# Two-layer hybrid decoder trunk: the steps from w_o to the layer's end in an order of their own for each engine, and the seven products in the order P1 P7 P2 P6 P3 P5 P4

## The chip, the core and the metric

One core of one Trainium2 chip runs the whole kernel. The metric is the device time of one execution, in microseconds (us). Below, PE is TensorE (matmuls), DVE is VectorE, ACT is ScalarE, SP is SyncE (it only issues transfers here).

## The reference

```python
for l in range(2):                                   # x: 512 tokens x 1024
    u = rms_norm(x, norm1_w[l])
    proj = u @ w_in[l]                               # projections of three branches, and gates
    ybr = stack([short_conv(...), gated_linear_attention(...), sliding_window_attention(...)])
    branch = einsum('bsgc,gcd->bsgd', ybr, w_branch[l])
    mixed = sum(sigmoid(gates) * branch, axis=2)
    x = x + mixed @ w_o[l]
    h = rms_norm(x, norm2_w[l])
    x = x + square(relu(h @ w_up[l])) @ w_down[l]    # w_up 1024 x 4096, w_down 4096 x 1024
```

All is float32. The change touches each layer from `mixed @ w_o` to its end.

## The kernel before

**Split products.** PE multiplies in a rounded 32-bit form. So each operand is split into a high part and the remainder, and each product is three matmuls: high by high, low by high, high by low. For every weight tile ACT writes the high part (`split_high`, L767) and then DVE the remainder (`split_low`, L984). A *unit* is the work on one such tile of 128x1024: 24 matmuls for a unit of w_up (`up0` to `up31` in a layer) or of w_o (`wa0`-`wa3`, `wb0`-`wb3`), 12 for one of w_down (`dn0` to `dn55`). The split tiles lie in four slots (`SPLIT`), so the split of a unit waits until the unit four before it is done, and PE waits for `lo_done` before each unit. Before, each engine's loop calls `split_ahead` at fixed places: at the step of unit n it splits unit n+3.

**The MLP.** The hidden width of 4096 is done in four quarters. In a quarter PE does eight `up` units (the hidden activations, transposed, one accumulator each) and then 14 `dn` units. ACT takes each `up` result through relu and square (L942, L944) and writes its high part; DVE writes the remainder (`hidden_low`). The product of a quarter's hidden activations with its 1024 rows of w_down is done by seven products of half-size blocks (a Winograd form of Strassen's scheme) in place of eight: for each product i (0 to 6 in the code) two units, one for each pair of w_down row blocks. Four of the weight operands are sums of blocks that DVE makes in place in `raw_down` (L1366): b12 = b22 - b12, b11 = b12 + b11, then b21 = b21 - b11, b11 = b22 - b11. Three of the left operands are sums of hidden blocks (`hidden_sums`: L1348, L1350, L1352, rounded by ACT in L930, remainders L1361) and one a difference (`hidden_diff`, L1342).

**The order of a quarter, before.** The products are taken in the order of i, so the units `dn2`, `dn3` are the second product. DVE makes b12 and b11 at the steps of up6 and up7, and b21 and b11 again at `dn2`, `dn3`. Each product's result is taken from its accumulators by `down_result` two units later: three products go to x directly (L1370, scaled by a norm factor for each token), four are kept over the quarters in `product_sums` (L1385, L1387) and are combined and added to x in the last quarter. All are lines of one loop for each engine; there is no scheduler. Within an engine's queue the instructions run in program order, and a wait holds all behind it.

**Banks.** Each product takes two of the four accumulators, the next product the other two; PE opens them again when DVE has taken the result of the product before the last.

**Transposes.** x is transposed on PE for the norms: V0-V7 between the attention part and the MLP (after `wb1` and after `up1`), UT4-UT7 for the next layer after the unit `dn54`.

**Transfers.** SP issues w_up in slabs of two units (1 MB, two slots, `raw_free`), and after the four slabs of a quarter the quarter's w_down: two halves (`down_full[0]`, `down_full[1]`) of two 1 MB transfers each, once `down_free` says that the last quarter's half has been split.

## Time and profile before

| what | value |
|---|---|
| median of the runs shown (3 runs, 1687.06 to 1688.86) | 1687.3 us |
| the profiled execution's own time | 1687.93 us |
| span of its trace | 1686.1 us |
| PE busy | 1604.5 us (95%) |
| DVE busy | 1060.4 us (63%) |
| ACT busy | 727.8 us (43%) |
| mean granted TensorE clock | 0.984 |
| DMA, mean over the span | 90 GB/s |

Busy times are shares of the span of the trace; the device time is 1.8 us longer. A matmul's record lasts longer than the distance to the next one (they are pipelined), so PE's progress is read from counts in a stretch, not from the duration of one.

### The profile page before, as it was taken

To read this page: it belongs to the slowest core of one execution; us is meant where nothing else is said; L and a number is where in the kernel's file an instruction comes from. 1 tells how busy PE (TensorE), PEld (TensorE's weight loads), DVE (VectorE), ACT (ScalarE), POOL (GpSimd) and SP (SyncE) were. 2 spreads that over 40 slices of the span, in tenths; PEclk is the share of its full clock that TensorE was granted. 3 is DMA by queue.
4 is the path that set the end of the run, shared out by engine and by line. 5 is a ranking of instruction groups with operands and counts; after the bars stand their busy time and mean duration, and the time that the engine had idled before them with its cause. 6 is when DMAs were issued, how large, how long until landed. Compare 5 with 4: busy or idle time off the path is not lost.

```text
span 1686.1 us, 20623 instructions
## 1 busy us (share of the span) xinstructions
PE 1604.5 (95%) x7488; PEld 1306.2 (77%) x7488; DVE 1060.4 (63%) x1508; ACT 727.8 (43%) x1128; POOL 0.2 (0%) x4
## 2 busy tenths in 40 slices
PE   6999999999998989999789999999999989898987
PEld 4878778888887877778577877788888868787875
DVE  4566774554548677675966666655455494857668
ACT  4546552322254453535345465432233544534451
POOL 0000000000000000000000000000000000000000
PEclk9999999999999999999999999999999999999999
DMA  4321222332341412214012213133223504040301
GB/s 142 104 97 51 75 76 76 100 123 77 108 169 48 146 54 100 101 50 155 1 58 93 76 52 99 51 100 125 75 75 125 196 5 175 25 175 25 141 10 50
DMA packets 107572, 151.09 MB, mean 90 GB/s; under 512 B 4912, under 2 KB 81232, under 8 KB 107472
## 3 DMA queue, kind: packets, MB, share of 16 engines
q1 hardware_dynamic: 107040, 149.69, 26.7%
q8 instruction: 60, 0.98, 0.2%
q14 instruction: 40, 0.33, 0.1%
q10 hardware_dynamic: 432, 0.08, 0.0%
HBM read 147.67 MB, written 2.10 MB: 89 GB/s over the span
## 4 chain that ended last, share of the span: by engine, by line
PE 78%; DVE 12%; ACT 4%; DVEq 2%; issue 2%; SPq 1%; DMA 0%; ACTq 0%
PE acc L478 17%; PE acc L479 16%; PE acc L480 16%; PE acc L500 5%; PE acc L502 5%; PE acc L501 5%; DVE raw_down L1366 4%; PE acc L527 3%; PE acc L528 3%; PE acc L529 3%; DVE wl_rows L984 3%; ACT wh_rows L767 2%; DVEq L1431 1%; DVE x_tokens L1370 1%; PE bank L664 1%
## 5 line engine op out<-in xcount | busy, mean ns | idle before, releaser
L478 PE MATMUL acc<-uh,wh 128*128 128x512 f32 x1152 | 453.6, 394 | 7.2 <-DVEq L1001 7.1
L480 PE MATMUL acc<-uh,wl 128*128 128x512 f32 x1152 | 449.5, 390 | 0.0
L479 PE MATMUL acc<-ul,wh 128*128 128x512 f32 x1152 | 449.5, 390 | 0.0
L984 DVE TENSOR_TENSOR wl<-raw,wh 128x1024 fp32r<-128x1024 f32 x144 | 176.3, 1225 | 171.7 <-ACT wh L767 163.7
L478 PEld LDWEIGHTS acc<-uh,wh 128*128 128x128 f32 x1152 | 216.9, 188 | 58.1 <-DVE wl L984 7.8
L480 PEld LDWEIGHTS acc<-uh,wl 128*128 128x128 f32 x1152 | 216.8, 188 | 45.9
L479 PEld LDWEIGHTS acc<-ul,wh 128*128 128x128 f32 x1152 | 216.9, 188 | 43.8
L767 ACT ACTIVATE wh<-raw 128x1024 fp32r<-128x1024 f32 x144 | 152.0, 1056 | 174.2 <-PE acc L480 83.9
L767 ACT ACTIVATE wh_rows<-raw_down 128x1024 fp32r<-128x1024 f32 x112 | 114.9, 1051 | 129.0 <-DVE raw_down L1366 69.6
L984 DVE TENSOR_TENSOR wl_rows<-raw_down,wh_rows 128x1024 fp32r<-128x1024 f32 x112 | 136.9, 1222 | 38.1 <-ACT wh_rows L767 34.8
L527 PE MATMUL acc<-wh_rows,hidden_hi 128*128 128x512 f32 x192 | 83.3, 434 | 37.3 <-DVE wl_rows L984 37.2
L1010 DVE TENSOR_TENSOR gate_tanh<-acc,rsqrt_rows 128x512 f32<-128x512 f32 x48 | 33.2, 691 | 115.7 <-PE acc L480 115.5
L500 PE MATMUL acc<-wh_rows,uh 128*128 128x512 f32 (+1 forms) x256 | 97.4, 381 | 6.7 <-DVE swa_qk_tokens L1098 6.4
L915 ACT ACTIVATE gate_tanh<-gate_tanh 128x512 f32<-128x512 f32 x40 | 25.3, 633 | 171.7 <-DVEq L1011 171.7
L502 PE MATMUL acc<-wl_rows,uh 128*128 128x512 f32 (+1 forms) x256 | 94.4, 369 | 0.0
L501 PE MATMUL acc<-wh_rows,ul 128*128 128x512 f32 (+1 forms) x256 | 94.3, 368 | 0.0
L942 ACT ACTIVATE hidden<-acc 128x512 f32<-128x512 f32 x64 | 38.3, 598 | 125.9 <-PE acc L480 125.9
L527 PE MATMUL acc<-wh_rows,hidden_sums_hi 128*128 128x512 f32 x192 | 77.1, 402 | 11.2 <-DVE x_tokens L1370 6.0
L1366 DVE TENSOR_TENSOR raw_down<-raw_down 128x1024 f32<-128x1024 f32 x64 | 78.4, 1225 | 6.1
L528 PE MATMUL acc<-wh_rows,hidden_lo 128*128 128x512 f32 x192 | 81.3, 423 | 0.0
L529 PE MATMUL acc<-wl_rows,hidden_hi 128*128 128x512 f32 x192 | 80.8, 421 | 0.0
L527 PEld LDWEIGHTS acc<-wh_rows,hidden_hi 128*128 128x128 f32 x192 | 40.0, 208 | 50.4 <-DVE wl_rows L984 41.0
(212 smaller groups left out, 2433.7 us busy)
## 6 DMA issues: line engine op xcount, KB each, us to landing
raw<-in_w_in_dram SPq DMA_DIRECT2D x40, 1024.0 KB, 5.2
raw<-in_w_up_dram SPq DMA_DIRECT2D x32, 1024.0 KB, 5.6
raw_down<-in_w_down_dram SPq DMA_DIRECT2D x32, 1024.0 KB, 11.1
raw_branch<-in_w_in_dram SPq DMA_DIRECT2D x12, 1024.0 KB, 5.0
raw_branch<-in_w_branch_dram SPq DMA_DIRECT2D x12, 1024.0 KB, 5.0
raw_branch<-in_w_o_dram SPq DMA_DIRECT2D x8, 1024.0 KB, 5.0
x_tokens<-in_x_dram SPq DMA_DIRECT2D x4, 512.0 KB, 5.2
raw_kv<-in_w_in_dram SPq DMA_DIRECT2D x4, 512.0 KB, 3.6
```

Of the source, the lines that this page charges most:

```text
L478: nc.tensor.matmul(a[:], wh[slot][:, k, :], right_h, start=at_k == 0, stop=False)
L479: nc.tensor.matmul(a[:], wh[slot][:, k, :], right_l, start=False, stop=False)
L480: last = nc.tensor.matmul(a[:], wl[slot][:, k, :], right_h, start=False, stop=at_k == n - 1)
L500: nc.tensor.matmul(to, left_h[:, k, s], h[:, row, 0:cols], start=k == 0, stop=False)
L501: nc.tensor.matmul(to, left_l[:, k, s], h[:, row, 0:cols], start=False, stop=False)
L502: last = nc.tensor.matmul(to, left_h[:, k, s], lo[:, row, 0:cols], start=False, stop=k == KT - 1)
L527: nc.tensor.matmul(to[:], left[0], h[:, row, :], start=k == 0, stop=False)
L528: nc.tensor.matmul(to[:], left[1], h[:, row, :], start=False, stop=False)
L529: last = nc.tensor.matmul(to[:], left[0], lo[:, row, :], start=False, stop=k == BK - 1)
L767: nc.scalar.activation(split_view(True, u), raw_view(u), ACT.Copy).then_inc(hi_done, 1)
L984: V.tensor_tensor(split_view(False, u), raw_view(u), split_view(True, u).bitcast(f32), ALU.subtract).then_inc(lo_done, 1)
L1366: return V.tensor_tensor(to, a, b, op)
```

## The change

The four loops of the late part are replaced by three written-out lists of steps (`PE_LATE`, `ACT_LATE`, `DVE_LATE`), which each engine walks on its own. In them `+u` is the split of unit u, `rl`/`hh` are relu with square and the high part, `hl` the remainder, `su`/`sh`/`sl` the sums of hidden blocks with their high and low part, `df`/`dh`/`dl` the same for the difference, `ta`, `tb`, `tc`, `td` the four sums of w_down blocks (for each half), `rs` the taking of one accumulator of a product, `fo` the combining of the kept sums, `ra`/`rb` the residual of w_o, `gc` a copy of an accumulator by ACT. A DVE step begins with a drain (the engine finishes what it has begun). The products run as i = 0, 4, 1, 2, 5, 3, 6. On SP the two halves of w_down are issued between the slabs of the quarter. The combining of the kept sums moves from the last quarter's results to its `up` steps, from sums without the last quarter, and the last products are then added to each of the x tiles that they belong to.

```diff
+PRODUCT = (0, 4, 1, 2, 5, 3, 6)
+PE_LATE = """wa0 wa1 wa2 wa3 wb0.01 V0 wb0.2 V1 wb0.3 V2 wb1.0 V3 wb1.123 wb2 wb3 up0.0 V4 up1.0 V5 up2.0 V6 up3.0 V7 up0.1 up1.1
...
+dn42 dn43 dn44 dn45 dn46 dn47 dn48 dn49 dn50 dn51 dn52 dn53 dn54 dn55.0 UT4 dn55.1 UT5 UT6 UT7""".split()
...
                     for i in range(8 * q, 8 * q + 8, 2):
                         load(l, f"up{i}", rows(w_up, l, 0, KT, i * P, SLAB_COLS))
-                    for pair in range(PAIRS):
-                        sp.wait_ge(down_free[pair], l * QUARTERS + q + 1)
...
+                        pair = i % 8 // 2 - 1
+                        if pair in range(PAIRS):
+                            sp.wait_ge(down_free[pair], l * QUARTERS + q + 1)
...
+                def fold(i):
+
+                    g1, g6, g5, g7 = (g[:] for g in gsum)
+                    if i == 1:
+                        V.tensor_tensor(g6, g6, g1, ALU.add)
+                        V.drain().then_inc(folded, 1)
+                    elif i == 3:
+                        V.tensor_tensor(g7, g7, g6, ALU.add)
+                    else:
+                        row, half, part = {0: (0, 0, g1), 2: (0, 1, g6), 4: (1, 1, g7), 5: (1, 0, g7),
+                                           6: (0, 1, g5), 7: (1, 1, g5)}[i]
+                        for t in range(2):
+                            scaled_into_x(row, t, half, part[:, t, :])
+
+                def down_last(place, t):
...
+                    if i == 0:
+                        dve.wait_ge(g1_ready, 2 * l + t + 1)
+                        scaled_into_x(0, t, 0, a[:]).then_inc(free, 1)
+                    elif i == 2:
+                        V.tensor_tensor(g1, g1, a[:], ALU.add).then_inc(free, 1)
+                        V.drain()
+                        for row, half in ((0, 1), (1, 1), (1, 0)):
+                            scaled_into_x(row, t, half, g1)
+                    else:
+                        tiles = {1: ((0, 0),), 3: ((0, 1), (1, 1)), 4: ((1, 1), (1, 0)), 5: ((0, 1),), 6: ((1, 0),)}[i]
+                        for row, half in tiles:
+                            last = scaled_into_x(row, t, half, a[:])
+                        last.then_inc(free, 1)
...
+                for word in DVE_LATE:
+                    kind, i = step_of(word)
                     V.drain()
```

In `DVE_LATE` the second quarter of a layer reads, from up15 to the start of the next quarter: `+up15 dl1 +dn14 tb2 su4 hl12 +dn15 tb3 su5 hl13 sl4 su6 hl14 sl5 +dn16 sl6 +dn17 su7 rs14 rs15 hl15 sl7 +dn18 +dn19 +dn20 rs16 rs17 +dn21 tc2 +dn22 rs18 rs19 td2 +dn23 tc3 td3 +dn24 rs20 rs21 +dn25 rs22 rs23 +dn26 +dn27 rs24 +up16`. The last quarter reads, from dn46 on: `+dn46 rs42 hl31 rs43 +dn47 +dn48 rs44 rs45 +dn49 sl15 +dn50 rs46 rs47 tc6 rs48 td6 +dn51 tc7 rs49 td7 +dn52 rs50 +dn53 +dn54 rs51 +dn55 rs52 rs53 +gq0 +gq1 +gk0 UT4 UT5 UT6 UT7 rs54 rs55`.

What stands in DVE's queue in the second quarter of the first layer, before: from the split of dn16 (`wl_rows_70`; the four slots are 70 to 73 in turn, `raw_down_127` and `128` are the two halves of w_down). The rows of hidden sums and remainders that repeat are left out.

```order
L984 TENSOR_TENSOR wl_rows_70<-raw_down_127,wh_rows_66 128x1024
L1366 TENSOR_TENSOR raw_down_128<-raw_down_128 128x2x512 x2
...
L1361 TENSOR_TENSOR hidden_sums_lo<-hidden_sums,hidden_sums_hi 128x768 x2
L984 TENSOR_TENSOR wl_rows_71<-raw_down_128,wh_rows_67 128x1024
L984 TENSOR_TENSOR wl_rows_72<-raw_down_127,wh_rows_68 128x1024
L1366 TENSOR_TENSOR raw_down_127<-raw_down_127 128x2x512 x2
L1387 TENSOR_TENSOR product_sums_122<-product_sums_122,acc 128x512 x2
L984 TENSOR_TENSOR wl_rows_73<-raw_down_128,wh_rows_69 128x1024
L1366 TENSOR_TENSOR raw_down_128<-raw_down_128 128x2x512 x2
```

The first row is the split of dn16, the next split (`wl_rows_71`) that of dn17; between them stand two block sums and all of the last three hidden blocks. The same place in the changed kernel, from the split of dn16 to that of dn22:

```order
L1013 TENSOR_TENSOR wl_rows_70<-raw_down_127,wh_rows_66 128x1024
L1453 TENSOR_TENSOR hidden_sums_lo<-hidden_sums,hidden_sums_hi 128x768
L1013 TENSOR_TENSOR wl_rows_71<-raw_down_128,wh_rows_67 128x1024
...
L1013 TENSOR_TENSOR wl_rows_72<-raw_down_127,wh_rows_68 128x1024
L1013 TENSOR_TENSOR wl_rows_73<-raw_down_128,wh_rows_69 128x1024
L1013 TENSOR_TENSOR wl_rows_70<-raw_down_127,wh_rows_66 128x1024
L1362 TENSOR_TENSOR product_sums_125<-product_sums_125,acc 128x512 x2
L1013 TENSOR_TENSOR wl_rows_71<-raw_down_128,wh_rows_67 128x1024
L1465 TENSOR_TENSOR raw_down_127<-raw_down_127 128x2x512
L1013 TENSOR_TENSOR wl_rows_72<-raw_down_127,wh_rows_68 128x1024
```

Only one remainder stands between the splits of dn16 and dn17 now, and of the second pair of block sums the first (L1465) comes between the splits of dn21 and dn22. The first block sum of a half, b12, is now made at the `up` steps.

DVE in the last quarter of the first layer, before, from the split of dn50 (`wl_rows_72`) to that of dn52 (`wl_rows_70`); `product_sums_122` to `125` are the four kept sums.

```order
L984 TENSOR_TENSOR wl_rows_72<-raw_down_127,wh_rows_68 128x1024
L1387 TENSOR_TENSOR product_sums_123<-product_sums_123,acc 128x512
L1370 SCALAR_TENSOR_TENSOR x_tokens<-product_sums_123,rsqrt_tokens_mlp_sq,x_tokens 128x512
L1396 TENSOR_TENSOR product_sums_125<-product_sums_125,product_sums_123 128x512
L1387 TENSOR_TENSOR product_sums_123<-product_sums_123,acc 128x512
L1370 SCALAR_TENSOR_TENSOR x_tokens<-product_sums_123,rsqrt_tokens_mlp_sq,x_tokens 128x512
L1396 TENSOR_TENSOR product_sums_125<-product_sums_125,product_sums_123 128x512
L984 TENSOR_TENSOR wl_rows_73<-raw_down_128,wh_rows_69 128x1024
L984 TENSOR_TENSOR wl_rows_70<-raw_down_127,wh_rows_66 128x1024
```

Between the splits of dn50 and dn51 stand the six operations of one product's result, and none between those of dn51 and dn52. The same place in the changed kernel, DVE again, from the split of dn50 to that of dn52:

```order
L1013 TENSOR_TENSOR wl_rows_72<-raw_down_127,wh_rows_68 128x1024
L1347 SCALAR_TENSOR_TENSOR x_tokens<-acc,rsqrt_tokens_mlp_sq,x_tokens 128x512 x2
L1465 TENSOR_TENSOR raw_down_127<-raw_down_127 128x2x512
L1387 TENSOR_TENSOR product_sums_122<-product_sums_122,acc 128x512
L1347 SCALAR_TENSOR_TENSOR x_tokens<-product_sums_122,rsqrt_tokens_mlp_sq,x_tokens 128x512 x3
L1467 TENSOR_TENSOR raw_down_127<-raw_down_127 128x2x512
L1013 TENSOR_TENSOR wl_rows_73<-raw_down_128,wh_rows_69 128x1024
L1465 TENSOR_TENSOR raw_down_128<-raw_down_128 128x2x512
L1387 TENSOR_TENSOR product_sums_122<-product_sums_122,acc 128x512
L1347 SCALAR_TENSOR_TENSOR x_tokens<-product_sums_122,rsqrt_tokens_mlp_sq,x_tokens 128x512 x3
L1467 TENSOR_TENSOR raw_down_128<-raw_down_128 128x2x512
L1013 TENSOR_TENSOR wl_rows_70<-raw_down_127,wh_rows_66 128x1024
```

Four block sums of 128x1024 (L1465, L1467), which stood ahead of these splits before, are now among them, with the ten operations of two results.

## Rows read from the trace of the kernel before

**Rows 1.** The page, part 1: PE's busy time, share and instructions.

```profile
PE 1604.5 (95%) x7488; PEld 1306.2 (77%) x7488; DVE 1060.4 (63%) x1508; ACT 727.8 (43%) x1128; POOL 0.2 (0%) x4
```

**Rows 2.** Who PE waited for: us in total, times, longest us.

```profile
PE acc L527 <- DVE wl_rows L984: 43.5, 15, 4.6
```

**Rows 3.** Stretches: us, busy (x instructions) of PE, PEld, DVE, ACT, POOL, PEclk, DMA, GB/s.

```profile
436.54:481.84 45.30, 45.30 (x209) 37.74 (x208) 23.10 (x26) 12.85 (x15) 0.00 (x0) 1.00 0.37 116
481.84:572.99 91.15, 85.83 (x377) 70.17 (x376) 65.36 (x87) 47.01 (x63) 0.00 (x0) 0.98 0.25 86
572.99:662.05 89.06, 84.02 (x361) 68.47 (x360) 60.72 (x71) 40.23 (x51) 0.00 (x0) 0.98 0.27 95
662.05:751.42 89.37, 83.81 (x361) 68.35 (x360) 60.71 (x71) 40.21 (x51) 0.00 (x0) 0.98 0.27 94
751.42:856.24 104.82, 91.10 (x377) 73.08 (x376) 76.20 (x91) 42.94 (x55) 0.00 (x0) 0.93 0.24 84
...
1315.49:1406.65 91.16, 85.65 (x377) 70.10 (x376) 65.37 (x87) 47.06 (x63) 0.00 (x0) 0.98 0.24 85
1406.65:1495.73 89.08, 84.76 (x362) 69.48 (x361) 60.63 (x71) 40.33 (x51) 0.00 (x0) 0.96 0.27 94
1495.73:1585.11 89.38, 84.74 (x362) 69.30 (x361) 60.72 (x71) 40.33 (x51) 0.00 (x0) 0.96 0.27 95
1585.11:1682.44 97.33, 86.37 (x361) 68.38 (x359) 69.51 (x84) 36.95 (x48) 0.00 (x0) 0.96 0.20 75
```

**Rows 4.** Stretches of two quarters: the up units, and the product units (columns as above).

```profile
572.99:616.51 43.52, 43.52 (x193) 36.04 (x192) 20.90 (x26) 22.16 (x32) 0.00 (x0) 1.00 0.52 185
616.51:662.05 45.54, 40.50 (x169) 32.43 (x168) 39.81 (x46) 18.06 (x20) 0.00 (x0) 0.96 0.04 9
...
794.94:856.24 61.30, 47.58 (x185) 37.04 (x184) 55.30 (x66) 20.78 (x24) 0.00 (x0) 0.89 0.03 9
```

**Rows 5.** Timeline of PE: start, us, line, operation, [idle before <-releaser].

```profile
540.06 0.50 PE L527 MATMUL acc<-wh_rows,hidden_hi 128*128 128x512 f32 x1 [4.61 <-DVE wl_rows L984]
...
821.85 0.47 PE L527 MATMUL acc<-wh_rows,hidden_sums_hi 128*128 128x512 f32 x1 [1.68 <-DVE x_tokens L1370]
...
849.10 0.45 PE L543 MATMUL bank<-consts,x_tokens 128*128 128x128 f32 x1 [4.59 <-DVEq L1405]
```

**Rows 6.** Stretches behind two of these waits (columns as in rows 3).

```profile
540.00:542.00 2.00, 1.94 (x6) 1.50 (x7) 1.77 (x3) 0.06 (x1) 0.00 (x0) 0.63 0.00 0
820.00:830.00 10.00, 8.32 (x37) 6.68 (x36) 8.95 (x12) 4.84 (x5) 0.00 (x0) 1.00 0.00 0
```

**Rows 7.** Timeline of DVE around the wait at 540.06.

```profile
535.42 0.42 DVE L1350 TENSOR_TENSOR hidden_sums<-hidden_sums,hidden 128x256 f32<-128x256 f32 x1
...
536.44 0.69 DVE L1355 TENSOR_TENSOR hidden_lo<-hidden,hidden_hi 128x512 fp32r<-128x512 f32 x1
537.05 1.82 DVE L1361 TENSOR_TENSOR hidden_sums_lo<-hidden_sums,hidden_sums_hi 128x768 fp32r<-128x768 f32 x2
538.79 2.53 DVE L984 TENSOR_TENSOR wl_rows<-raw_down,wh_rows 128x1024 fp32r<-128x1024 f32 x2
541.46 2.52 DVE L1366 TENSOR_TENSOR raw_down<-raw_down 128x1024 f32<-128x1024 f32 x2
543.90 1.28 DVE L1385 COPY product_sums<-acc 128x512 f32<-128x512 f32 x2
545.10 1.21 DVE L984 TENSOR_TENSOR wl_rows<-raw_down,wh_rows 128x1024 fp32r<-128x1024 f32 x1
...
550.22 1.41 DVE L1370 SCALAR_TENSOR_TENSOR x_tokens<-acc,rsqrt_tokens_mlp_sq,x_tokens 128x512 f32<-128x512 f32 x2
```

**Rows 8.** Groups of instructions by line and form: busy us, mean ns of one.

```profile
L767 ACT ACTIVATE wh_rows<-raw_down 128x1024 fp32r<-128x1024 f32 x112 | 114.9, 1051 | 129.0 <-DVE raw_down L1366 69.6 <-PE acc L529 59.3
L942 ACT ACTIVATE hidden<-acc 128x512 f32<-128x512 f32 x64 | 38.3, 598 | 125.9 <-PE acc L480 125.9
L944 ACT ACTIVATE hidden<-hidden 128x512 f32<-128x512 f32 x64 | 40.5, 633 | 5.2
```

**Rows 9.** The page, part 6, transfers: line engine op xcount, KB each, us to landing.

```profile
raw_down<-in_w_down_dram SPq DMA_DIRECT2D x32, 1024.0 KB, 11.1
```

394 lines of the change are left out of this document (195 added, 199 removed).

## The prediction

> **What bounds the kernel now.** I read the page first: PE is busy 95% of the span [rows 1], so only what keeps PE from starting matmuls can move the end. Second, PE's waits: the largest is for DVE's remainders of w_down tiles, 43.5 us in 15 waits [rows 2]. Third, where they lie. In the up units of a quarter 192 matmuls take 43.52 us [rows 4], 0.2267 us each: that is PE without a wait. So an up unit takes 5.44 us and a dn unit of 12 matmuls 2.72 us, and a quarter (8 and 14 of them, 360 matmuls) would take 81.6 us. It takes 89.06 and 89.37 us in the middle of a layer [rows 3]: 7.46 and 7.77 us lost, all among the dn units (45.54 us for 38.08 us of matmuls [rows 4]). The first quarter has 16 transposes more. Their price is in the row of w_o, 45.30 us for 192 matmuls and 16 transposes [rows 3], so 45.30 - 43.52 = 1.78 us; then 91.15 - 81.6 - 1.78 = 7.77 us are lost. In all, the six quarters that are not a layer's last lose 7.77 + 7.46 + 7.77 + 7.78 + 7.48 + 7.78 = 46.0 us. The last quarters take 104.82 (with 16 transposes) and 97.33 us [rows 3]: 21.4 and 15.7 us lost.
>
> The timeline shows why. PE stands 4.61 us before `dn3` at 540.06 [rows 5], and DVE has no pause there: sums, remainders and splits follow each other [rows 7]. A quarter's dn part holds 39.81 us of DVE work in 45.54 us, its up part only 20.90 in 43.52 [rows 4]. So the bound is an uneven load on DVE: too much work stands before the splits of dn2 and dn3. Behind the wait the granted clock is 0.63 in 540 to 542 [rows 6], so it has gone down to 1.2 GHz for a part of it; `dn3` then takes 4.67 us (540.06 to 544.73, the last matmul's slot included) in place of 2.72, 1.95 us more. Behind a wait of 1.68 us the clock stays at 1.00 [rows 5, 6].
>
> **The change, costed by walking the two queues.** Durations from the rows. A DVE operation on 128x1024 behind a drain starts 1.31 us after the one before ([rows 7]: two splits at 538.79, the next at 541.46); the drain thus adds 0.085 to 1.225. So I take 0.77 us for one accumulator's copy or add, 0.51 for each step of a hidden sum, 0.77 for a remainder of 128x512, 1.03 for one of a hidden sum, 0.83 for a scaled addition to x (1.49 for two in a row). An ACT split is 1.05 us [rows 8], 1.1 with its drain; relu and square 0.60 and 0.63 [rows 8], 1.4 together.
>
> *A middle quarter*, from the first matmul of up8 = 0. PE without waits ends up15 at 43.5 and starts dn14+j at 43.5 + 2.72 j. Until dn16 DVE is early: the list has b12 (`ta2`, `ta3`) among the up units. The chain that sets the rest: up15 ends 43.5, ACT splits dn17, relu and square until 46.0, DVE's `su7` until 47.5, then the results of the first product (its second tile is done with dn15 at 49.0) until 49.8, `hl15` 50.6, `sl7` 51.6, and three splits in a row, dn18 52.9, dn19 54.2, dn20 55.5. PE wants these at 54.4, 57.1, 59.8. On with the list: two results 57.1, dn21 58.4, `tc2` 59.7, dn22 61.0 (wanted 65.3), two results 62.6, `td2` 63.9, dn23 65.2, `tc3` `td3` 67.8, dn24 69.1 (wanted 70.7), results 70.7, dn25 72.0 (73.4), results 73.6, dn26 74.9 (76.2), dn27 76.2 (78.9), then up16 78.3 (81.6). No split is late, the smallest margin is 1.3 to 1.6 us. The accumulators are taken in time too: the sixth product opens its first at 70.7, where `rs20` ended at 69.9. The other five non-last quarters give the same by the same walk (in the first, `hl7` ends at 52.7 where dn5 wants it at 59.0). So 46.0 us go.
>
> *A last quarter.* Its results cost more: 24 additions of one tile in the dn part and twelve half-rows plus two adds of 128x1024 among the up units, where there is room. By the walk DVE has dn46 at 49.3 (wanted 54.4), dn48 at 54.4 (59.8), dn50 at 61.0 (65.3). Then two results 62.7, `tc6` 64.0, one result of add and three scaled additions (0.77 + 0.66 + 0.66 + 0.83 = 2.9) 67.0, `td6` 68.3, dn51 69.7: wanted 68.0, **1.7 us late**. `tc7` 71.0, the second such result 73.9, `td7` 75.2, dn52 76.5: PE would now want it at 72.4, **4.1 us late**. All later splits are in time. So 5.8 us of waits, and as 4.1 is near the 4.61 behind which the clock fell, I add its 1.95 us: the quarter takes 81.6 + 5.8 + 1.95 = 89.3 us. In layer 1 that is 97.33 - 89.3 = 8.0 us won. In layer 0 the transposes add 1.78 and the first unit of the next layer waits some 0.4 for the remainders of UT5 to UT7: 104.82 - 91.5 = 13.3 us won; the wait of 4.59 us before the transposes at 849.10 [rows 5] goes, since DVE ends the last right-hand x tile at 85.5 in my walk and PE reaches the transposes at 88.
>
> *Against it*: the groups of 16 transposes are cut into fours, each return to 128x512 matmuls costs about 0.1 us (1.78 / 16 = 0.11 for all of a transpose is the upper bound), 12 more returns: 1.2 us. Below it is nothing. I take 1.2.
>
> *At nothing*: more drains on ACT (727.8 us busy of 1686 [rows 1]; its queue is waited for only where DVE is not late); 1.0 us for the two `gc` copies, hidden before dn47; the earlier issue of the w_down halves. Four 1 MB transfers in a row land in 11.1 us each [rows 9]; the second half is issued about 1.6 us before up8 starts and so lands by 9.5, while `ta3` is reached at about 9 and holds the split of up13, wanted at 5 x 5.44 = 27.2. With 1.31 us for `ta3` and 1.31 for the split a landing up to 24.6 costs nothing: a cover of 15 us.
>
> *The sum*: 46.0 + 8.0 + 13.3 - 1.2 = 66.1 us. 1686.1 - 66.1 = 1620.0 us of span, plus the 1.8 us between span and device time 1621.8; the profiled run is 0.6 us above the median, so **1621 us**.
>
> **A rule weighed.** In the list each accumulator is taken as a step of its own behind a drain; before, the two of a product ran in a row, both done 1.20 us after the first began (543.90, the next split at 545.10 [rows 7]), 0.60 us each. With drains I count 0.77, so 14 x 0.17 = 2.4 us more DVE work in a quarter. The Trainium skill (VectorE: DVE Perf Modes, "The DRAIN you can't avoid") says the pipe is flushed after every operation anyway and that leaving out waits between them wins nothing. By it the list's drains would be free: about 2.4 us less lateness in each last quarter, 1616 us in place of 1621. The row speaks against it, so I keep 0.77.
>
> **The rivals.**
> - *A: the last quarters lose little.* Should DVE be some 2.4 us earlier than in my walk, the wait at dn52 is under 2 us and the clock stays up, as at 821.85. Then each last quarter gains 2.4 + 1.95 = 4.35 us more: 1621 - 8.7 = 1612 us. For it: the margins are sums of twenty terms, and one that is 0.1 too large makes 2 us. Against: the terms are measured.
> - *B: short waits in every quarter.* The margins of 1.3 us in the middle quarters are of the same size as that error. If every one of the six keeps a wait of 2 us and half of a fall of the clock with it, they lose 6 x 3, and a last quarter 3 more each: 1621 + 24 = 1645 us.
> - *C: slower.* The queue of DVE holds `ta3` ahead of the splits of up13 and up14. If the second half of w_down landed late, all splits behind would be late. It costs nothing up to a landing 24.6 us after the quarter starts, and the change loses as much as it wins (66 / 8 = 8.2 us in each quarter) at 32.8. Landing at 36 would give 1687 + 8 x 3.2 = 1713 us. Against it: 24.6 is far above the 9.5 expected, with the DMA engines 0.52 busy in the up part [rows 4].
> - *D: no change.* If the waits were due to something that the lists keep (PE's own start behind `lo_done`), the time stays near 1687. Rows 7 show DVE without a pause there, so hardly.
>
> **How the numbers follow.** The forecast (1615 to 1628) 0.50, A and below 0.20, B 0.24, C 0.03, D 0.03. The time predicted is the forecast's. The range 1608 to 1640 takes in A with both last quarters good, and most of B: what lies outside is a quarter of B, a part of A, C and D, under 0.2. A measurement of this kernel tells a change from none at about 0.2% (3.4 us). Faster by more: forecast, A and B, 0.94; same 0.02, most of D; slower 0.04, C and the rest of D.
>
> **What the profile after would show.** Right: stretches of 360 matmuls in 81.6 to 82 us between the first up units of two middle quarters, with no wait for `wl_rows` and the clock at 1.00 in them; in the last quarter two waits, before dn51 and dn52; no wait before UT4. DVE's busy time in the up part goes up, in the dn part down. The prediction is wrong if a middle quarter still shows waits (B), if PE waits before an up unit with DVE standing at the first sum of w_down blocks (C), or if a last quarter's dn part takes 38 to 40 us (A).

## The result, and the profile after

The changed kernel takes 1625.72 us (median of 4 runs, 1625.26 to 1626.25) against 1687.22 us (1687.06 to 1688.86) before: a ratio of 0.9634, with a 95% interval of 0.9617 to 0.9650. The forecast was 1621 us, the range 1608 to 1640. The profiled execution took 1625.36 us, its span 1623.6. The steps have the same names; only line numbers moved (a split on VectorE is L1013 now, a product's matmuls L570 to L572, `tc` L1465, `td` L1467, a scaled addition to x L1347).

The page, part 1, then PE's waits of the whole span (us in total, times, longest us), answering to [rows 1, 2]:

```profile
PE 1584.9 (98%) x7488; PEld 1296.4 (80%) x7488; DVE 1088.6 (67%) x1524; ACT 745.5 (46%) x1132; POOL 0.2 (0%) x4
```

```profile
PE acc L570 <- DVE wl_rows L1013: 11.2, 4, 3.9
PE bank L587 <- DMA x_tokens<-in_x_dram: 9.9, 1, 9.9
PE acc L520 <- DVEq L1030: 7.2, 1, 7.2
...
PE acc L570 <- DVE product_sums L1360: 0.2, 1, 0.2
```

Fifteen waits of 43.5 us for the remainders of w_down blocks have become four of 11.2. The next two rows are of the start of the program, before the first product (9.93 to 20.62 us). Gone are also six waits for results that VectorE had not yet taken from their accumulators; PE's waits before:

```profile
PE acc L527 <- DVE x_tokens L1370: 6.0, 6, 1.7
```

PE's own busy time went down too, by 19.6 us; fewer matmuls at the low clock were part of it (the mean granted clock is 0.992 in this execution).

The stretches that answer to [rows 3] (w_o and the four quarters of layer 0, then the quarters of layer 1):

```profile
436.02:481.44 45.42, 45.42 (x210) 37.62 (x209) 24.52 (x27) 15.28 (x18) 0.00 (x0) 1.00 0.56 193
481.44:565.24 83.80, 83.80 (x378) 69.06 (x377) 64.72 (x85) 47.36 (x61) 0.00 (x0) 1.00 0.22 72
565.24:646.84 81.60, 81.60 (x362) 67.59 (x361) 62.74 (x71) 41.87 (x51) 0.00 (x0) 1.00 0.30 101
646.84:728.64 81.80, 81.80 (x361) 67.51 (x360) 62.32 (x71) 41.88 (x51) 0.00 (x0) 1.00 0.31 107
728.64:821.63 92.99, 86.78 (x377) 71.03 (x376) 82.73 (x96) 44.44 (x55) 0.00 (x0) 0.96 0.22 74
...
1282.28:1366.27 83.99, 83.79 (x378) 69.05 (x376) 64.71 (x86) 47.35 (x61) 0.00 (x0) 1.00 0.22 72
1366.27:1447.87 81.60, 81.60 (x362) 67.57 (x360) 62.76 (x71) 41.85 (x51) 0.00 (x0) 1.00 0.30 101
1447.87:1530.03 82.16, 82.12 (x362) 67.41 (x360) 62.81 (x71) 41.88 (x51) 0.00 (x0) 1.00 0.31 105
1530.03:1620.13 90.10, 85.09 (x361) 69.37 (x359) 78.56 (x93) 39.89 (x50) 0.00 (x0) 0.96 0.18 64
```

Two quarters are exactly 360 matmuls long, 81.60 us, with the clock at 1.00 and PE busy all the time. The halves of the second and of the last quarter of layer 0 show how the work moved (compare [rows 4]):

```profile
565.24:608.76 43.52, 43.52 (x194) 36.05 (x193) 28.21 (x35) 24.28 (x33) 0.00 (x0) 1.00 0.44 146
608.76:646.84 38.08, 38.08 (x170) 31.54 (x169) 34.53 (x37) 17.59 (x18) 0.00 (x0) 1.00 0.14 50
728.64:772.16 43.52, 43.52 (x193) 36.04 (x192) 39.41 (x48) 24.21 (x33) 0.00 (x0) 1.00 0.45 148
772.16:821.63 49.47, 43.26 (x185) 34.99 (x184) 43.33 (x48) 20.22 (x23) 0.00 (x0) 0.93 0.03 8
```

VectorE has 28.21 us of work among the up units where it had 20.90, and 34.53 among the product units where it had 39.81. That is 3.5 us less than the 38.08 us that PE's matmuls take: it fits.

The last quarter has the two waits that were expected, before dn51 and dn52. PE's timeline, then VectorE's, then the clock in stretches (columns as in rows 3):

```profile
799.15 0.50 PE L570 MATMUL acc<-wh_rows,hidden_sums_hi 128*128 128x512 f32 x1 [2.35 <-DVE wl_rows L1013]
...
806.03 0.80 PE L570 MATMUL acc<-wh_rows,hidden_sums_hi 128*128 128x512 f32 x1 [3.86 <-DVE wl_rows L1013]
806.63 0.63 PE L571 MATMUL acc<-wh_rows,hidden_sums_lo 128*128 128x512 f32 x1
```

```profile
797.87 1.23 DVE L1013 TENSOR_TENSOR wl_rows<-raw_down,wh_rows 128x1024 fp32r<-128x1024 f32 x1
799.19 1.23 DVE L1465 TENSOR_TENSOR raw_down<-raw_down 128x1024 f32<-128x1024 f32 x1
800.50 0.69 DVE L1387 TENSOR_TENSOR product_sums<-product_sums,acc 128x512 f32<-128x512 f32 x1
801.28 2.08 DVE L1347 SCALAR_TENSOR_TENSOR x_tokens<-product_sums,rsqrt_tokens_mlp_sq,x_tokens 128x512 f32<-128x512 f32 x3
803.44 1.23 DVE L1467 TENSOR_TENSOR raw_down<-raw_down 128x1024 f32<-128x1024 f32 x1
804.75 1.23 DVE L1013 TENSOR_TENSOR wl_rows<-raw_down,wh_rows 128x1024 fp32r<-128x1024 f32 x1
```

```profile
804.00:806.00 2.00, 0.00 (x0) 0.00 (x0) 1.89 (x2) 1.17 (x2) 0.00 (x0) 0.78 0.00 0
806.00:808.00 2.00, 1.97 (x5) 1.58 (x6) 1.84 (x2) 1.86 (x2) 0.00 (x0) 0.50 0.00 0
808.00:810.00 2.00, 2.00 (x6) 1.56 (x5) 1.81 (x3) 0.14 (x1) 0.00 (x0) 0.50 0.00 0
810.00:812.00 2.00, 2.00 (x6) 1.57 (x5) 1.52 (x2) 0.38 (x1) 0.00 (x0) 0.51 0.00 0
812.00:814.00 2.00, 2.00 (x10) 1.64 (x10) 0.81 (x2) 0.68 (x1) 0.00 (x0) 1.00 0.00 0
```

Between the splits of dn51 (797.87) and dn52 (804.75) VectorE has no pause: `tc7`, the result `rs49` with its three scaled additions, `td7`. PE stands 3.86 us, the granted clock falls to 0.50 (1.2 GHz), and the next matmuls are 0.63 us long where they would be 0.39 or 0.40.

### The profile page after: what moved, and what is told of

Same layout as the page of the kernel before. It is cut to its first block, busy times and chain, and to the rows that moved or that the text cites. A ratio compares the mean times of both kernels' runs of the same rounds, so it can differ in the third digit from the quotient of the medians.

```text
span 1623.6 us, 21215 instructions
## 1 busy us (share of the span) xinstructions
PE 1584.9 (98%) x7488; PEld 1296.4 (80%) x7488; DVE 1088.6 (67%) x1524; ACT 745.5 (46%) x1132; POOL 0.2 (0%) x4
## 4 chain that ended last, share of the span: by engine, by line
PE 92%; DVE 5%; ACT 1%; DVEq 1%; SPq 1%; issue 0%; DMA 0%; ACTq 0%
PE acc L520 19%; PE acc L522 19%; PE acc L521 19%; PE acc L570 5%; PE acc L572 5%; PE acc L571 5%; PE acc L542 5%; PE acc L544 5%; PE acc L543 5%; DVE wl_rows L1013 2%; PE bank L708 1%; PE bank L727 1%; DVE x_tokens L1347 1%; PE bank L587 1%; PE bank L719 1%; PE bank L666 1%
## 5 line engine op out<-in xcount | busy, mean ns | idle before, releaser
L521 PEld LDWEIGHTS acc<-ul,wh 128*128 128x128 f32 x1152 | 216.8, 188 | 43.5
L1013 DVE TENSOR_TENSOR wl<-raw,wh 128x1024 fp32r<-128x1024 f32 x144 | 176.3, 1225 | 68.7 <-ACT wh L799 57.4
L799 ACT ACTIVATE wh_rows<-raw_down 128x1024 fp32r<-128x1024 f32 x112 | 118.9, 1061 | 153.1 <-DVE raw_down L1467 65.7
L1013 DVE TENSOR_TENSOR wl_rows<-raw_down,wh_rows 128x1024 fp32r<-128x1024 f32 x112 | 137.2, 1225 | 15.8 <-ACT wh_rows L799 6.1
L570 PE MATMUL acc<-wh_rows,hidden_sums_hi 128*128 128x512 f32 x192 | 78.1, 407 | 11.4 <-DVE wl_rows L1013 11.2
L799 ACT ACTIVATE wh_rows<-raw_branch 128x1024 fp32r<-128x1024 f32 x40 | 42.3, 1059 | 76.3 <-PE acc L544 66.4
L571 PE MATMUL acc<-wh_rows,hidden_sums_lo 128*128 128x512 f32 x192 | 76.8, 400 | 0.0
L572 PE MATMUL acc<-wl_rows,hidden_sums_hi 128*128 128x512 f32 x192 | 76.7, 399 | 0.0
L570 PE MATMUL acc<-wh_rows,hidden_hi 128*128 128x512 f32 x192 | 75.0, 390 | 0.0
L572 PE MATMUL acc<-wl_rows,hidden_hi 128*128 128x512 f32 x192 | 74.7, 389 | 0.0
L571 PE MATMUL acc<-wh_rows,hidden_lo 128*128 128x512 f32 x192 | 74.7, 389 | 0.0
```

Source lines behind the costliest of these rows:

```text
L521: nc.tensor.matmul(a[:], wh[slot][:, k, :], right_l, start=False, stop=False)
L570: nc.tensor.matmul(to[:], left[0], h[:, row, :], start=k == 0, stop=False)
L571: nc.tensor.matmul(to[:], left[1], h[:, row, :], start=False, stop=False)
L572: last = nc.tensor.matmul(to[:], left[0], lo[:, row, :], start=False, stop=k == BK - 1)
L799: nc.scalar.activation(split_view(True, u), raw_view(u), ACT.Copy).then_inc(hi_done, 1)
L1013: V.tensor_tensor(split_view(False, u), raw_view(u), split_view(True, u).bitcast(f32), ALU.subtract).then_inc(lo_done, 1)
```

## The experiments

Each kernel is the changed one with the edit shown. Where a median is given, it is of four or five runs, or more, on a chip on which the kernel before was timed as well (1687.5 to 1687.8 us). e1 to e4 were timed on one chip, e5 to e8 on a second, e9 and e10 on a third, e11 and e12 on a fourth. The median of the kernel before differs by up to 0.6 us between them and the result above, so a difference of less than 1 us between kernels of different chips says nothing. For each run the table has the time from PE's first matmul of one unit to that of the next, for layer 0: the first three quarters, the last one up to dn55, and from dn55 to `gq0` of layer 1. In the kernel before and in e4 the 16 transposes stand ahead of dn55, in the others behind its start, so for these two only the sum of the last two columns can be compared.

```
kernel                     median us   up0-up8  up8-up16  up16-up24  up24-dn55  dn55-gq0
before                      1687.22     91.15     89.06     89.37     100.98      3.84
changed                     1625.72     83.80     81.60     81.80      88.43      4.56
e1 old transfer order       1647.84     83.80     82.39     83.76      97.35      4.56
e2 b12 sums late            1642.70     86.42     83.62     83.95      89.38      4.55
e3 old product order        1668.39     92.02     85.50     87.81      90.55      4.75
e4 old places               1688.22     92.08     89.95     90.25      97.58      3.51
e5 transposes in groups     1625.82     84.05     81.60     81.80      87.16      4.55
e6 no drain between rs      1623.33     83.52     81.60     81.60      87.35      4.51
e7 additions behind dn55    1621.60     83.78     81.60     81.80      81.38      7.43
e8 e6 and e7                1619.47     83.52     81.61     81.60      81.49      7.54
e9 additions spread         1619.90     83.53     81.60     81.60      81.49      6.10
e10 split of gq0 first      1621.35     83.52     81.60     81.60      81.49      7.72
e11 one sum                 1616.40     83.52     81.60     81.60      81.53      6.21
e12 splits sooner           1617.11     83.52     81.60     81.60      81.16      6.79
```

**e1: the old order of transfers.** SP again issues all four w_down transfers of a quarter in one place, behind the quarter's four slabs. In the first quarter of each layer `ta0` and `ta1` had to follow them, from their early places to behind `+up4`; all other sums stay where they are.

```diff
-                        pair = i % 8 // 2 - 1
-                        if pair in range(PAIRS):
-                            sp.wait_ge(down_free[pair], l * QUARTERS + q + 1)
...
+                    for pair in range(PAIRS):
+                        sp.wait_ge(down_free[pair], l * QUARTERS + q + 1)
...
```

> The changed kernel with the w_down halves issued after all four slabs of a quarter, as before; in each layer's first quarter the two b12 sums stand behind the split of up4, since the slab they would wait behind is issued only then. Theory (the place of DVE's work between the splits sets the waits): the b12 sums wait some 10 us for their data among the up units, where DVE has over 20 us of room, and nothing reaches PE: 1625 to 1628 us. Rival (the earlier transfers are a part of the gain): at least 1 us a quarter, 1634 us or more.

Measured: 1647.84 us (ratio to before 0.9767, 0.9753 to 0.9782), 22 us more than the changed kernel. The theory missed, the rival is right: the issue of the transfers is a part of the change that earns something. VectorE's waits in the last quarter of layer 0, then its timeline:

```profile
DVE raw_down L1461 <- DMA raw_down<-in_w_down_dram: 10.6, 2, 10.1
```

```profile
737.35 1.23 DVE L1368 TENSOR_TENSOR product_sums<-product_sums,product_sums 128x1024 f32<-128x1024 f32 x1
748.68 1.23 DVE L1461 TENSOR_TENSOR raw_down<-raw_down 128x1024 f32<-128x1024 f32 x1 [10.11 <-DMA raw_down<-in_w_down_dram]
```

VectorE stands 10.11 us at `ta6`, in the up part, for a landing. Over the whole span it waits 74.0 us there in 13 waits; in the changed kernel 6.9 us in 6. PE does not see it at that place, where it has splits ahead (up24 to dn42 still take 43.54 us). It sees it from dn44 on, 34 us after VectorE's wait has ended. PE's timeline:

```profile
782.84 0.50 PE L570 MATMUL acc<-wh_rows,hidden_diff_hi 128*128 128x512 f32 x1 [2.26 <-DVE wl_rows L1013]
...
787.10 0.50 PE L570 MATMUL acc<-wh_rows,hidden_diff_hi 128*128 128x512 f32 x1 [2.59 <-ACT hidden L972]
```

The folds and remainders behind VectorE's wait slid into the product part (51.40 us of VectorE work in 774.98 to 832.00, where the changed kernel has 43.33 in 772.16 to 821.63). The granted clock is low for a part of 788 to 792 us (matmuls of 0.63 us), which belongs to the price. The quarter is 8.9 us longer. In the other quarters, where the two queues have more room, such waits cost 0 to 2.0 us. So this is the forecast's rival C, the sum that holds the queue, at a smaller price and in another place: PE waited for no split of an up unit in that quarter. The 22 us are the price of the old transfers beside early sums; no run has the old transfers beside the late sums of e2.

**e2: the b12 sums late.** Each `ta` stands directly ahead of its `tb`; the transfers keep the new order.

```diff
-ta2 ... ta3 ... tb2 ... tb3
+... ta2 tb2 ... ta3 tb3
```

> The changed kernel with the b12 sums not among the up units but right before the b11 sums, where they stood before: 2.6 us more of DVE work ahead of the splits of dn2 and dn3 in each quarter. Theory: the smallest margin of 1.3 to 1.6 us is used up, some 1 us of waits in each of the six other quarters, 2.6 us or more in each last quarter: 1633 to 1641 us. Rival (the product order does it, the sums have room): 1626 to 1628 us.

Measured: 1642.70 us (0.9738, 0.9722 to 0.9754), 17 us more, just above the 1633 to 1641 that the theory gave. The six quarters that are not a layer's last lose 2.0 to 2.6 us each, twice what the theory gave them, and the last ones 1.0 and 2.2. Two operations of 1.3 us moved into the product part are 2.6 us of work, and nearly all of it comes through to PE: VectorE has next to no spare time there. The theory named waits for splits (0.8 to 1.0 us before the third product in the first two quarters of a layer); the larger part stands before the sixth product, for an accumulator that VectorE takes late (0.8 to 2.1 us).

**e3: the old order of products** (P1 P2 P3 P4 P5 P6 P7), with the steps of each product moved along in VectorE's list.

```diff
-PRODUCT = (0, 4, 1, 2, 5, 3, 6)
+PRODUCT = (0, 1, 2, 3, 4, 5, 6)
```

> The changed kernel with the products in the order 0 1 2 3 4 5 6 as before; DVE's list is rewritten where it must be, with the second pair of block sums between the splits of dn5 and dn7. Theory (only with the product order is there room for the block sums): all four sums of a quarter must stand ahead of the splits of the fourth product, the walk gives its second split 3.4 us late, with a fall of the clock in some quarters: 1650 to 1670 us. Rival (the list alone does it, in whatever product order): 1626 to 1632 us.

Measured: 1668.39 us (0.9884, 0.9866 to 0.9901), within the theory's range. VectorE's timeline in the second quarter of layer 0:

```profile
635.23 1.22 DVE L1466 TENSOR_TENSOR raw_down<-raw_down 128x1024 f32<-128x1024 f32 x1
636.54 1.23 DVE L1468 TENSOR_TENSOR raw_down<-raw_down 128x1024 f32<-128x1024 f32 x1
638.89 1.22 DVE L1014 TENSOR_TENSOR wl_rows<-raw_down,wh_rows 128x1024 fp32r<-128x1024 f32 x1 [1.12 <-ACT wh_rows L800]
```

The blocks made by `tc` and `td` are wanted by the very next split, so ScalarE's copy (1.06 us) and VectorE's remainder run one after another, and PE waits 2.73 us at dn21, the second unit of the fourth product; that unit starts 3.0 us late, where the theory said 3.4. What the theory did not name: before the fourth product's first unit PE waits another 0.44 to 2.54 us, quarter by quarter, for an accumulator. With the new order other splits lie between a sum and its use.

**e4: the old places.** New product order and transfers, but every step of the three lists stands where the loops before had it (a split three units ahead, `ta` and `tb` together behind the splits of dn1 and dn2, `tc` and `td` behind those of dn7 and dn8).

```diff
-... hl28 +dn43 tb7 su13 hl29 sl12 +dn44 ...
+... every step by the old loops' rule
```

> The changed kernel with new product order, transfers and the combining among the up units, but with the steps of all three engines at their old places (three units ahead, b12 and b11 at the steps of up6 and up7, all hidden sums before the split of dn3, results two units later). Theory: the wait of 4.3 to 4.6 us before dn3 with the fall of the clock is back in every quarter, the smaller wait before dn6 is not: 6 quarters at 6.3 us, last quarters about as now: 1660 to 1672 us. Rival (the product order does it): 1640 us or less.

Measured: 1688.22 us (1.0004, 0.9995 to 1.0014). Neither number of the expectation holds: at the old places the new order of products earns nothing, with the new transfers and the combining among the up units beside it. The first of these rows is of PE in the second quarter, the others of VectorE and ScalarE ahead of it:

```profile
630.44 0.80 PE L571 MATMUL acc<-wh_rows,hidden_diff_hi 128*128 128x512 f32 x1 [5.79 <-DVE wl_rows L1014]
```

```profile
627.06 2.01 DVE L1454 TENSOR_TENSOR hidden_sums_lo<-hidden_sums,hidden_sums_hi 128x768 fp32r<-128x768 f32 x2
629.16 2.54 DVE L1014 TENSOR_TENSOR wl_rows<-raw_down,wh_rows 128x1024 fp32r<-128x1024 f32 x2
```

```profile
626.22 0.84 ACT L986 ACTIVATE hidden_sums_hi<-hidden_sums 128x768 fp32r<-128x768 f32 x1 [2.50 <-DVE hidden_sums L1450]
627.20 4.63 ACT L800 ACTIVATE wh_rows<-raw_down 128x1024 fp32r<-128x1024 f32 x4
```

ScalarE's copies of four blocks stand behind a hidden sum for which ScalarE waits 2.50 us, and VectorE's splits behind the same sums. So the theory had the place right: the wait is back where it was before the change ([rows 5]: 4.61 us before dn3), at the second unit of the second product, in every quarter, with a fall of the clock behind it. It had the size too small. The wait is 5.67 to 6.29 us where it was 4.32 to 4.61 before, and with the clock it costs 7.5 to 8.9 us in each of the six quarters and not 6.3. Why it is longer than before is not shown; the steps of the lists have more drains than the old loops, and no run tests that.

**e5: the transposes in groups.** V0 to V3 behind wb1, V4 to V7 behind up1's first half. UT4 to UT7 stand between the halves of dn55 in the kernel that ran, not ahead of dn55 as the expectation says.

```diff
-dn54 dn55.0 UT4 dn55.1 UT5 UT6 UT7
+dn54 dn55.0 UT4 UT5 UT6 UT7 dn55.1
```

> The changed kernel, but the transposes stand in two groups of four again (V0-V3 behind wb1, V4-V7 behind up1's first half, UT4-UT7 ahead of dn55), where the change had them one at a time between products. It prices the 1.2 us that the prediction added for the transposes cut in fours. Theory (each step between two parts of a unit costs TensorE some 0.1 us): about 1.2 us faster than the changed kernel, 1624.5 us. Rival (the split only moves a wait that DVE sets anyway, or hides one): no difference, or slower by up to 3 us where four transposes in a row wait for their copies one after another.

Measured: 1625.82 us (0.9634, 0.9621 to 0.9647), the rival: no difference. w_o is 0.12 us shorter (45.30 as in [rows 3]), the first quarter 0.25 us longer in layer 0 and 0.53 in layer 1.

**e6: no drain between neighbouring result steps.**

```diff
-                    V.drain()
+                    if not (kind == last_kind == "rs"):
+                        V.drain()
+                    last_kind = kind
```

> The changed kernel, but where two steps that fold a finished accumulator into the results stand directly behind each other in VectorE's order (rs, rs), the drain between them is left out. By the rows, two drained steps start 0.77 us apart and undrained ones 0.70 to 0.75 us with the drain's share gone (0.60 by the nearest row), so VectorE has up to 2.4 us less to do in each w_down part, and dn51 and dn52 of the last quarters stand less long: together 3 to 6 us, 1620 to 1622.5 us. Rival, by the rule of the Trainium skill, VectorE: DVE Perf Modes, the section on the drain that can't be avoided (the pipeline drains between operations anyway): no difference from the changed kernel, 1625.5 us within 0.7.

Measured: 1623.33 us (0.9621, 0.9608 to 0.9634), 2.4 us less than the changed kernel and between the two expectations. A pair of results, in the changed kernel and then in e6 (VectorE's timelines):

```profile
621.11 1.47 DVE L1362 TENSOR_TENSOR product_sums<-product_sums,acc 128x512 f32<-128x512 f32 x2
```

```profile
620.75 1.28 DVE L1362 TENSOR_TENSOR product_sums<-product_sums,acc 128x512 f32<-128x512 f32 x2
```

A pair takes 0.19 us less; two scaled additions take 1.41 us in place of 1.59. That is the price of one drain, which the forecast took as 0.17. By the Trainium skill (VectorE: DVE Perf Modes, "The DRAIN you can't avoid") leaving out waits between operations wins nothing, though the same section says that a next operation that is not held starts earlier. Here leaving out the drain wins 0.18 to 0.19 us a pair, so for these operations the row was right. The expectation's 2.4 us for a quarter was too much by its own rows: only the drain inside a pair goes, four to six in a quarter, some 0.7 to 1.1 us. In the last quarter two of them stand ahead of the split of dn52. There nothing came through: in layer 0, dn51 to dn52 takes 6.89 us where it took 6.88. From `tc6` to the split of dn52 no two result steps are neighbours. `tc6` itself starts at 791.65 in place of 792.30; 0.41 us of this is PE's own earlier start, and behind the next sum a pause of 0.44 us, for which the trace shows no releaser, takes the rest. The gain of the two traces is made of the small waits of the first and third quarters (0.28 and 0.20 us in layer 0, 0.36 and 0.56 in layer 1), of 1.2 us less in the matmuls from dn52 on in layer 0 (a shorter fall of the clock), and of 0.5 us around them in layer 1. The first part, 1.4 us, is the drains'. The shorter fall may be chance: the same unit's fall costs 1.5 to 2.6 us in ten cases (last section).

**e7: the additions of product 2 behind dn55.** In the last quarter the step only adds the accumulator to the kept sum and frees it; its six scaled additions are steps `gx0`, `gx1` of their own. The edit moves some neighbours too: `rs51` stands one split earlier, UT4 to UT7 all stand behind dn55 on PE, and the splits of `gq1` and `gk0` stand behind them on ScalarE and VectorE.

```diff
                     elif i == 2:
                         V.tensor_tensor(g1, g1, a[:], ALU.add).then_inc(free, 1)
-                        V.drain()
-                        for row, half in ((0, 1), (1, 1), (1, 0)):
-                            scaled_into_x(row, t, half, g1)
-+dn52 rs50 +dn53 +dn54 rs51 +dn55 rs52 rs53 +gq0
++dn52 rs50 +dn53 rs51 +dn54 +dn55 gx0 gx1 rs52 rs53 +gq0
```

> The changed kernel, but in the last quarter of each layer the step that folds product 2 only adds the accumulator to the partial sum, which frees the accumulator; its three scaled additions per half go to VectorE behind +dn55, when it has time. The transposes of the layer's end follow dn55. Theory (in the last quarter VectorE's own order sets the end: dn51 and dn52 wait for splits that stand behind these six additions, 4.2 us of work, and the 4 us wait for dn52 makes the clock fall): dn52 is at most 1.5 us late, the granted clock stays at 1.00 around it, the last quarter of layer 0 takes 5 to 6 us less, that of layer 1 4 to 5 us less: 1613 to 1617 us. Rival (VectorE is not what holds the last quarter, the late w_down blocks are, or the work moved behind dn55 comes back as a wait at the start of the next layer and in the tail): 1621 to 1626 us, and in layer 1 a tail longer than 3.5 us.

Measured: 1621.60 us (0.9610, 0.9597 to 0.9623), 4.1 us less. PE's two waits of the last quarter in layer 0, and the clock behind the second:

```profile
797.78 0.50 PE L571 MATMUL acc<-wh_rows,hidden_sums_hi 128*128 128x512 f32 x1 [0.17 <-DVE wl_rows L1014]
...
802.51 0.50 PE L571 MATMUL acc<-wh_rows,hidden_sums_hi 128*128 128x512 f32 x1 [1.72 <-DVE wl_rows L1014]
```

```profile
802.00:804.00 2.00, 1.49 (x6) 1.23 (x7) 1.82 (x3) 1.73 (x3) 0.00 (x0) 1.00 0.00 0
804.00:806.00 2.00, 2.00 (x10) 1.66 (x9) 1.82 (x3) 0.98 (x2) 0.00 (x0) 1.00 0.00 0
```

Theory and rival are each half right. Behind a wait of 1.72 us the clock stays at 1.00, and up24 to dn55 takes 7.05 us less in layer 0 (6.02 in layer 1): more than expected. But the moved additions stand ahead of the transposes now: 

```profile
808.18 4.23 DVE L1348 SCALAR_TENSOR_TENSOR x_tokens<-product_sums,rsqrt_tokens_mlp_sq,x_tokens 128x512 f32<-128x512 f32 x6
812.49 1.41 DVE L1348 SCALAR_TENSOR_TENSOR x_tokens<-acc,rsqrt_tokens_mlp_sq,x_tokens 128x512 f32<-128x512 f32 x2
```

From dn55 to `gq0` takes 2.87 us more, from `gq0` to `kva0` 2.2 us more, and in layer 1 from dn55 to the end of the span 9.87 us where it was 6.16. So 13.1 us were won and 8.8 given back.

**e8: both**, the edits of e6 and e7, with no further one.

> The additions moved behind dn55 and the drains left out between neighbouring result steps, together. Theory (VectorE's lateness in the last quarter is the only stop left, so what each saves adds only until dn51 and dn52 have no wait): 1611 to 1616 us, at least 0.5 us under the kernel with the moved additions alone. Rival (the drain costs nothing beside neighbouring operations): the same as with the moved additions alone within 0.5 us.

Measured: 1619.47 us (0.9598, 0.9585 to 0.9611), 2.1 us under e7: with the theory in that it is over 0.5 us less, and above its 1611 to 1616. The drains are worth the same 2 us with and without the long waits of the last quarter, so their gain lies elsewhere: the small waits of 1.4 us in the first and third quarters go here too.

**e9: the additions spread**, on top of e8. `gx0` and `gx1` now make the two additions of each half that the transposes need, `gx2` and `gx3` the third.

```diff
-+dn52 rs50 +dn53 rs51 +dn54 +dn55 gx0 gx1 rs52 rs53 +gq0 UT4 UT5 UT6 UT7 +gq1 +gk0 rs54 rs55
++dn52 rs50 +dn53 rs51 +dn54 gx0 +dn55 gx1 rs52 rs53 +gq0 UT4 UT5 UT6 UT7 +gq1 gx2 gx3 rs54 rs55 +gk0
```

> As the kernel with moved additions and without the drains between result steps, but the additions are not left in one block behind dn55. The two per half that the next transposes need stand one pair behind the split of dn54 and one pair behind that of dn55, where the trace of that kernel shows VectorE 3 us ahead of TensorE; the third of each half (column half 0 of rows 1) stands behind the transposes, with the last result steps. Theory (what was won in the last quarter came back because four more microseconds of additions stood between dn55 and the transposes): the transposes start 1.3 to 1.6 us sooner, in layer 0 and, for the outputs, in the tail, and 1 to 3 us are won in all: 1616.5 to 1618.5 us. Rival (the start of the next layer waits for the copies of the transposes and for the weight splits anyway, and 2.9 us of additions behind them hold up UT0 to UT3): 1619 to 1621 us.

Measured: 1619.90 us (0.9598, 0.9585 to 0.9611), the rival's time. The transposes do start sooner (dn55 to `gq0` 6.10 us in place of 7.54), but the tail, where `gx2` and `gx3` stand directly ahead of the last results, takes 10.87 us in place of 9.42: what one end of a layer wins, the other loses, in the same list.

**e10: the split of gq0 first**, on top of e9.

```diff
-+dn55 gx1 rs52 rs53 +gq0 UT4 UT5 UT6 UT7 +gq1 gx2 gx3 rs54 rs55 +gk0
++dn55 gx1 +gq0 rs52 rs53 UT4 UT5 UT6 UT7 gx2 gx3 +gq1 rs54 rs55 +gk0
```

> As the kernel with the additions spread, but the weight split of gq0 stands ahead of the last two result steps, and the third additions ahead of the split of gq1. Theory (the transposes wait for the result steps, so 1.3 us of split ahead of them is 1.3 us lost unless the steps wait for dn53 anyway): the same as the kernel with the additions spread within 0.7 us, or up to 1.3 us slower per layer end. Rival (the first product of the next layer waits for the split of gq0): 1 to 2 us faster than it.

Measured: 1621.35 us (0.9611, 0.9598 to 0.9624), 1.4 us more than e9; the rival is wrong. dn55 to `gq0` is 1.6 us longer: the transposes wait for the results, as the theory has it, and `gq1` then waits for its own split (`gq0` to `gq1` 5.67 us in place of 4.28).

**e11: one sum for two results.** On top of e8, product 3's accumulator is added to the kept product 2 and the sum goes once into each half of the rows: eight operations where there were ten, and the two that only `rs54` and `rs55` need come last.

```diff
+                    elif i == 3:
+                        g = gsum[2][:, t, :]
+                        V.tensor_tensor(g, g1, a[:], ALU.add).then_inc(free, 1)
+                        V.drain()
+                        for row in range(2):
+                            scaled_into_x(row, t, 1, g)
-+dn55 gx0 gx1 rs52 rs53 +gq0
++dn55 rs52 rs53 gx0 gx1 +gq0
```

> As the kernel with moved additions and without the drains between result steps, with less VectorE work at the end of each layer: product 3's accumulator is added to the kept product 2 in one sum of its own (freeing the accumulator), and that sum goes once into rows 0 and once into rows 1, in place of four scaled additions per half; the kept product 2 goes by itself only into rows 1, column half 0, behind those steps. Ten operations become eight, and two of them leave the way to the transposes. Theory (VectorE's queue from dn52 on is the end of the layer): the transposes start 1.5 to 2.2 us sooner in layer 0, and the tail is 1 to 1.8 us shorter: 1615.5 to 1617.5 us. Rival (the start of the next layer and the landing of the outputs wait for something else): 1619 to 1620 us.

Measured: 1616.40 us (0.9580, 0.9567 to 0.9593), within the theory's range, the fastest kernel of this study: 9.3 us under the changed one. Against e8, dn55 to `gq0` takes 1.33 us less (the theory said 1.5 to 2.2), `gq0` to `kva0` 1.0 us less, and dn55 to the end of the span 8.32 us in place of 9.42.

**e12: the splits of dn51 and dn52 ahead of the sums of pair 1**, on top of e11.

```diff
-tc6 rs48 td6 +dn51 tc7 rs49 td7 +dn52 rs50 +dn53
+tc6 td6 +dn51 rs48 +dn52 rs49 tc7 td7 rs50 +dn53
```

> As the kernel with one sum, but in the last quarter the splits of dn51 and dn52, which need only the sums of pair 0, stand ahead of the sums of pair 1, which dn53 is the first to need: tc6 td6 +dn51 rs48 +dn52 rs49 tc7 td7 rs50 +dn53. Theory: dn51 starts on time (2.72 us behind dn50), dn52 too or at most 0.3 us late, and dn53 is 1 to 2 us late instead of dn52; since VectorE stays full to the end, only 0.3 to 0.8 us is won per layer: 0.5 to 1.6 us under the kernel with one sum. Rival (the wait only changes its place): the same within 0.4 us.

Measured: 1617.11 us (0.9584, 0.9571 to 0.9597), 0.7 us more than e11; the runs of the two overlap (1616.98 to 1617.23, and 1615.70 to 1617.23), so only the gain of the theory can be ruled out. The theory had the places right: dn51 and dn52 start on time (2.72 us each), and dn53 is then 2.1 us late (4.86 us behind dn52). The rival says why nothing is won: the wait changed its place and kept its size, since VectorE is full up to there. The 0.37 us that the last quarter takes less in each layer comes back behind dn55 (0.58 us in layer 0, 0.56 in layer 1).

## Why the prediction held, and where it was off

- **Six quarters give 46.0 us.** They gave 44.25 (7.35, 7.46, 7.57, 7.17, 7.48 and 7.22). The walk was right unit by unit: two of them are exact. What is missing is in the first quarters (16 transposes in smaller groups: 83.52 us are left in e6, 0.14 above the 83.38 of 81.60 and 1.78) and waits of 0.2 to 0.6 us in four quarters, 1.4 us in all, which e6 removes. Rival B does not hold. e2 shows how near it was: 2.6 us more work in the product part makes 2.0 to 2.6 us of wait. The walk's 1.31 us for an operation on 128x1024 is a little under its own row (2.67 us for two splits in [rows 7]); the changed kernel shows 1.31 and 1.32.
- **The last quarter: 1.7 us late at dn51, 4.1 at dn52.** From start to start dn51 is 2.51 us late and dn52 4.16 in layer 0, 2.49 and 4.52 in layer 1. The place and the mechanism are right, and e7 shows that the six additions ahead of the two splits make the most of it (2.01 us are left at dn52). The two together were taken 0.9 us too small in layer 0 and 1.2 in layer 1. The walk has no term for pauses of VectorE of 0.16 to 0.43 us in which it waits for nothing that the trace shows, or just for an accumulator; most stand at operations that take one. Between dn42 and the split of dn52 they add up to 0.68 us in layer 0 and 1.11 in layer 1, most of what is missing.
- **The fall of the clock, 1.95 us.** dn52 and dn53 took 2.88 us too long in layer 0 and 1.49 in layer 1: mis-sized in both, 2.2 on average. In layer 1 the clock is low in dn51 too (its first matmul takes 0.79 us), but this is hidden, since dn52 starts when its split is done. The quarters are 92.99 us = 81.60 + 2.51 + 4.16 + 2.88 + 1.84 for the transposes (forecast 91.5 with what follows), and 90.10 us = 81.60 + 2.49 + 4.52 + 1.49 (forecast 89.3). They gave 11.83 and 7.23 us in place of 13.3 and 8.0.
- **Transposes cut into fours, 1.2 us against it.** w_o takes 0.12 us more in each layer; e5, with groups, is no faster. With 0.14 us in each first quarter that makes 0.5 us; the term should have been nearer the middle of its bounds, nothing and 1.2 us.
- **Earlier transfers at nothing, with a cover of 15 us.** Right for the changed kernel (6.9 us of VectorE waits in all, and PE waits for no split but those of dn51 and dn52). But the step says nothing on how much depends on it: e1 shows 22 us. The forecast looked for the price of the new order and not for that of the old one beside early sums.
- **What had no term**: the front of layer 1, from `gq0` to w_o, takes 1.28 us more (415.23 for 413.95): remainders of UT6 and UT7 and the last results now stand beside the first units of the next layer. The start of the program is 0.52 us and the tail 0.26 us shorter.
- **The sum**: 44.25 + 11.83 + 7.23 + 0.52 + 0.26 - 1.28 - 0.24 (w_o) = 62.6 us of span, where 66.1 were forecast. The other 1.2 us of the distance from 1621 to 1625.72 are in the steps from span to median and in rounding: the forecast took 0.6 us off for the distance of the profiled run from the median before, and the changed kernel's profiled run is 0.4 us under its median. No two large errors cancel: every term but that of the transposes was forecast too favourable.
- **The rule weighed.** A drain does cost what the forecast took (0.17 us; 0.19 and 0.18 in e6). Whether 14 of them make a last quarter 2.4 us late is not tested: e6 leaves out two ahead of the split of dn52, 0.4 us at most. There `tc6` is 0.24 us earlier against PE. In the changed kernel the second result ahead of it waits 0.18 us for PE to finish the accumulator, so time saved before that point is only in part time won. The 1616 us given for the rule also leave the clock's fall in, which rival A takes out for the same 2.4 us (1612). Rival A wanted 4.35 us in each last quarter from an earlier VectorE; e7 got 7.05 and 6.02 by taking work from just that place.

Together e1 to e4 say that the gain has no single part: undoing the early b12 sums costs 17 us, the transfers 22, the product order 43 and the places of all steps 62 (which takes in the first). That is 144 in all, where 61.5 were won. Early sums need early transfers, and the late sums need the new product order that puts other splits between a sum and its use.

## What to carry to other kernels

Where two engines feed a third in order, write down for every step when it is wanted, and walk both queues with the trace's durations. It gave the place of the two large waits, and the size of each to about 1 us; it did not give the small waits of 0.2 to 0.6 us, nor the front of the next layer. A step that moves in such a list is paid for at each place that the list serves: work taken from before dn52 came back ahead of the transposes and in the tail, and only less work (e11), not other places (e9, e10, e12), won more. A wait on a queue with slack is no proof that it is free: in e1 VectorE's 10 us in the up part became PE's 9 us in the product part, from 34 us later on.
